# Index scores as three fp32r products instead of one fp32 product, in a hybrid encoder layer on one Trainium2 core

## The chip, the cores and the metric

The kernel runs on one core of one Trainium2 chip. The metric is the device time of one execution in microseconds (us). TensorE is the matrix engine, VectorE, ScalarE and GpSimd compute element by element, and SyncE (SP) issues most of the DMA transfers. "PEld" in the profile is TensorE's weight load, which can overlap its matmuls.

## What is computed

One inference step of one layer on 1,024 prompt tokens and 128 sample tokens (8 sequences of 16). The reference, cut to what matters:

```python
h = RMSNorm_pre(x) * (1 + scale) + shift
z = h @ W_in                      # (1152, 2048) @ (2048, 5712)
q, k, v, iq, ik, iw, za, u, zs = split(z)
# indexer, block of 128 queries; 16 heads of 64; limit is block-causal by 64 tokens
s = einsum('bqhd,bsd->bqhs', iq, ik) * 64 ** -0.5
score = einsum('bqhs,bqh->bqs', relu(s), iw)
score = where(visible, score, -inf)
_, idx = top_k(score, 256)
# grouped-query attention over the chosen keys
attn = softmax(q @ gather(k, idx)) @ gather(v, idx)
# S5: 64 groups, 64 complex states each, scan over positions, y = Re(C h) + D u
y_ssm = gelu(s5(u)); y_ssm = y_ssm * sigmoid(y_ssm @ w_glu + b_glu)
out = concat(attn * silu(za), y_ssm * silu(zs)) @ W_out
y = x + gate * RMSNorm_post(out)
```

Queries among the first 256 tokens see at most 256 keys and need no choice, so index scores are computed for the query tiles 2 to 7 (tiles of 128 tokens), each against the keys up to its own end.

## The kernel before, in words

The program has two parts, `project_in` (about the first two thirds of the time) and `mix_tokens`. Only `project_in` is changed.

**The projection.** W_in is cut into 45 blocks of up to 128 output columns. Tokens go in two passes: the first has 768 tokens (two slices of 384), the second 384 tokens (one slice). The weights of a block come in two halves of 8 contraction blocks. So the work is a list of 180 half-blocks, called halves here: numbers 0 to 89 are the first pass, and NA = 90 to NA+89 the second. Every product of the projection is split: three fp32r matmuls, high by high, low by high and high by low (lines 1598 to 1600), 48 in a half of the first pass and 24 in one of the second. ScalarE copies a weight half to fp32r (`high`, line 983), VectorE subtracts that copy from the weights (`low`, line 1259); GpSimd does the subtraction in part of the second pass (line 817, `POOL_LOW`). In the first pass the split of half n+1 stands at the head of half n's work on ScalarE and VectorE, in the second the split of half n+2.

**What runs beside it.** Each engine goes through the same loop over halves and does extra work at fixed numbers. TensorE inserts work behind given products (`beside`, "spots"). The order is written by hand, as constants:

- `TILE_AT[t] = (first half, how many)` places index tile t. In its first halves TensorE does the score products, a pair of heads at a spot: 5 spots a half in the first pass (behind products 1, 4, 7, 10, 13) and 3 in the second (1, 4, 7). A pair is two heads on the upper and the lower 64 rows of the array (`score_pair`, line 1672), each in its own PSUM bank `ps_s`. ScalarE takes the relu (`relu`, line 1012) into one of two places of `rel`, VectorE multiplies by the head's weight and adds it to `score` (`add_scores`, lines 1420 and 1423). The remaining halves of the tile are for the search: 32 rounds of MAX8 and MATCH_REPLACE8 on VectorE (`choose`, lines 1435 and 1437) share them evenly (`rounds_in`), and a mask is kept at the end (line 1442).
- A score matmul waits until the unit two before it has had its relu. A relu waits until the unit two before it has been added.
- Eight batches of the scan run in the second pass, from half NA+7 on, one in 6 halves (`scan_at`). Batch b has its inputs multiplied in its halves 0 and 1 (line 1696), VectorE turns and scans them (lines 1221 to 1252), and its outputs are multiplied in halves 6 and 7 (lines 1715 and 1720). Tables `toep` and `q_mat` for the outputs are in two buffers and are loaded by `load_outputs` at offset 7 of the batch; inputs, with `p_in` and `rot`, by `load_inputs` at offset 5.
- SP issues the loads of the weights. Its iteration n starts once the half whose buffer it takes is done: 4 halves behind n in the first pass, 8 in the second. All other DMAs stand between them, in the same queue.
- The keys and values needed by the next part are loaded by `load_results` after half NA+71's weights and turned by TensorE in halves NA+70, NA+72 and so on (`turn_rows`).

The fp32 score matmul shows in the trace as two matmul records with two weight loads.

## Time and profile before

| | |
|---|---|
| median of 3 runs | 2257.27 us (2253.56 to 2257.91) |
| the profiled execution's own time | 2255.91 us |
| span of the profiled execution | 2254.0 us |
| TensorE busy | 2150.6 us, 95% |
| VectorE busy | 1268.4 us, 56% |
| ScalarE busy | 737.4 us, 33% |
| GpSimd busy | 449.0 us, 20% |
| first pass, halves 2 to 89 | about 120 to 977 us of the span |
| second pass, halves NA to NA+89 | 977 to 1486 us |
| score matmuls | 352 records, between 411 and 1380 us |

Times in the rows are microseconds from the span's start unless marked ns. A timeline row gives the start, the duration, engine, line, operation and tiles; "x4" at its end merges four instructions, and brackets hold the idle time before it and what ended it. Matmuls are pipelined, so a record's duration is longer than its distance from the next. Granted clock is that of TensorE, as a share of full speed.

### The profile page before, as it was taken

To read this page: it belongs to the slowest core of one execution; us is meant where nothing else is said; L and a number is where in the kernel's file an instruction comes from. 1 tells how busy PE (TensorE), PEld (TensorE's weight loads), DVE (VectorE), ACT (ScalarE), POOL (GpSimd) and SP (SyncE) were. 2 spreads that over 40 slices of the span, in tenths; PEclk is the share of its full clock that TensorE was granted. 3 is DMA by queue.
4 is the path that set the end of the run, shared out by engine and by line. 5 is a ranking of instruction groups with operands and counts; after the bars stand their busy time and mean duration, and the time that the engine had idled before them with its cause. 6 is when DMAs were issued, how large, how long until landed. Compare 5 with 4: busy or idle time off the path is not lost. (4 is left out here: it accounts for less than half of the span.)

```text
span 2254.0 us, 33185 instructions
## 1 busy us (share of the span) xinstructions
PE 2150.6 (95%) x13028; PEld 1869.8 (83%) x13028; DVE 1268.4 (56%) x2292; ACT 737.4 (33%) x1324; POOL 449.0 (20%) x654
## 2 busy tenths in 40 slices
PE   5899999999999998999999999989999989999898
PEld 3489999888898898999976977979777777887786
DVE  4228433577778693335547988955567553223353
ACT  5221222222322323332223234553355542222241
POOL 0001332792000000203333445620000000000100
PEclk9999999999999999999999999999999999999999
DMA  9954556344454335377764645544411222224653
GB/s 368 379 116 108 151 156 172 99 117 117 128 129 114 98 112 174 87 183 211 222 216 127 179 117 174 164 136 134 109 50 48 87 72 87 77 80 151 232 182 117
DMA packets 432381, 325.80 MB, mean 145 GB/s; under 512 B 122937, under 2 KB 377441, under 8 KB 430681
## 3 DMA queue, kind: packets, MB, share of 16 engines
q1 hardware_dynamic: 427618, 303.75, 46.4%
q0 software_dynamic: 4176, 16.78, 2.1%
q10 hardware_dynamic: 432, 3.15, 0.4%
q8 instruction: 104, 1.70, 0.3%
q14 instruction: 51, 0.42, 0.1%
HBM read 264.52 MB, written 63.28 MB: 145 GB/s over the span
## 5 line engine op out<-in xcount | busy, mean ns | idle before, releaser
L1598 PE MATMUL ps_z<-h_hi_a,w_hi 128*128 128x384 f32 (+1 forms) x1408 | 484.5, 344 | 1.4 <-DVE w_lo L1259 1.4
L1600 PE MATMUL ps_z<-h_hi_a,w_lo 128*128 128x384 f32 (+1 forms) x1408 | 472.5, 336 | 0.0
L1599 PE MATMUL ps_z<-h_lo_a,w_hi 128*128 128x384 f32 (+1 forms) x1408 | 471.5, 335 | 0.0
L1259 DVE TENSOR_TENSOR w_lo<-w_raw,w_hi 128x1024 fp32r<-128x1024 f32 (+1 forms) x135 | 185.0, 1374 | 362.1 <-ACT w_hi L983 361.6
L1598 PEld LDWEIGHTS ps_z<-h_hi_a,w_hi 128*128 128x128 f32 (+1 forms) x1408 | 263.2, 187 | 32.3 <-issue 27.1
L1599 PEld LDWEIGHTS ps_z<-h_lo_a,w_hi 128*128 128x128 f32 (+1 forms) x1408 | 263.5, 187 | 0.8
L1600 PEld LDWEIGHTS ps_z<-h_hi_a,w_lo 128*128 128x128 f32 (+1 forms) x1408 | 263.2, 187 | 0.9
L983 ACT ACTIVATE w_hi<-w_raw 128x1024 fp32r<-128x1024 f32 (+1 forms) x180 | 186.2, 1052 | 228.6 <-PE ps_z L1600 223.0
L1598 PE MATMUL ps_z<-h_hi_b,w_hi 128*128 128x384 f32 (+1 forms) x720 | 251.1, 349 | 0.6 <-DVE w_lo L1259 0.4
L1600 PE MATMUL ps_z<-h_hi_b,w_lo 128*128 128x384 f32 (+1 forms) x720 | 242.9, 337 | 0.0
L1599 PE MATMUL ps_z<-h_lo_b,w_hi 128*128 128x384 f32 (+1 forms) x720 | 242.6, 337 | 0.0
L2789 DVE TENSOR_TENSOR o_lo<-o_raw,o_hi 128x512 fp32r<-128x512 f32 x114 | 78.6, 691 | 220.3 <-ACT o_hi L2733 220.2
L1003 ACT ACTIVATE z_sb<-ps_z 128x384 f32<-128x384 f32 (+1 forms) x85 | 50.9, 600 | 343.1 <-PE ps_z L1600 343.1
L1598 PEld LDWEIGHTS ps_z<-h_hi_b,w_hi 128*128 128x128 f32 (+1 forms) x720 | 135.7, 188 | 32.4 <-issue 28.1
L2733 ACT ACTIVATE o_hi<-o_raw 128x512 fp32r<-128x512 f32 x114 | 71.7, 631 | 247.2 <-PE ps_l L2937 96.9
L817 POOL TENSOR_TENSOR w_lo<-w_raw,w_hi 128x1024 fp32r<-128x1024 f32 x45 | 110.8, 2465 | 175.4 <-ACT w_hi L983 175.4
L1599 PEld LDWEIGHTS ps_z<-h_lo_b,w_hi 128*128 128x128 f32 (+1 forms) x720 | 135.9, 189 | 0.4
L1600 PEld LDWEIGHTS ps_z<-h_hi_b,w_lo 128*128 128x128 f32 (+1 forms) x720 | 135.8, 189 | 0.4
L1435 DVE MAX8 top<-score_a 128x8 f32<-128x384 f32 (+3 forms) x128 | 97.2, 759 | 3.4
L1423 DVE SCALAR_TENSOR_TENSOR score_a<-rel_a,iw,score_a 128x384 f32<-128x384 f32 (+2 forms) x105 | 67.0, 639 | 50.0 <-ACT rel_a L1012 43.8
L1437 DVE MATCH_REPLACE8 score_a<-top,score_a 128x384 f32<-128x384 f32 (+3 forms) x128 | 95.0, 742 | 0.0
L826 POOL TENSOR_TENSOR z_sb<-z_sb,sig_a 128x768 f32<-128x768 f32 x16 | 29.5, 1842 | 315.8 <-ACT sig_a L1001 315.8
(508 smaller groups left out, 3848.2 us busy)
## 6 DMA issues: line engine op xcount, KB each, us to landing
w_raw<-in_w_in SPq DMA_DIRECT2D x176, 512.0 KB, 4.1
wada<-in_w_ada SPq DMA_DIRECT2D x32, 1024.0 KB, 14.2
o_raw<-in_w_out SPq DMA_DIRECT2D x114, 256.0 KB, 3.0
wg<-in_w_ada SPq DMA_DIRECT2D x32, 512.0 KB, 6.3
zt<-z_sb SPq DMA_DIRECT2D x36, 384.0 KB, 4.7
slabs<-in_x_prompt POOLq DMA_DIRECT2D x8, 1024.0 KB, 7.8
zt<-z_sb SPq DMA_DIRECT2D x36, 192.0 KB, 4.0
out_y_prompt<-out_rows POOLq DMA_DIRECT2D x10, 512.0 KB, 4.8
```

The source lines that it names most:

```text
L817: G.tensor_tensor(w_lo[r][:, :, 0:m], w_raw[r][:, :, 0:m], w_hi[s][:, :, 0:m].bitcast(F32), ALU.subtract).then_inc(w_lo_pool, 1)
L983: A(w_hi[s][:, :, 0:m], w_raw[r][:, :, 0:m], ACT.Copy).then_inc(w_hi_ok, 1)
L1003: A(dst, src, ACT.Copy).then_inc(z_read, 1)
L1259: V.tensor_tensor(w_lo[r][:, :, 0:m], w_raw[r][:, :, 0:m], w_hi[s][:, :, 0:m].bitcast(F32), ALU.subtract).then_inc(w_lo_ok, 1)
L1423: V.scalar_tensor_tensor(out, rel(t)[:, u % 2, 0:w], wgt, out, ALU.mult, ALU.add).then_inc(s_acc, 1)
L1435: V.max(top8[:], score(t)[:, 0:keys]).then_inc(top, 1)
L1437: V.match_replace(score(t)[:, 0:keys], top8[:], score(t)[:, 0:keys], CHOSEN).then_inc(top, 1)
L1598: M(out, hi, H_HI[p][:, kk, cols], start=kk == 0, stop=False)
L1599: M(out, hi, H_LO[p][:, kk, cols], start=False, stop=False)
L1600: return M(out, lo, H_HI[p][:, kk, cols], start=False, stop=kk == KB - 1)
L2733: A(hi, raw, ACT.Copy).then_inc(w_hi_ok, 1)
L2789: V.tensor_tensor(lo, raw, hi.bitcast(F32), ALU.subtract).then_inc(w_lo_ok, 1)
```

## The change

Three things are changed together.

1. The index scores of the prompt are computed as the projection's products are: queries and keys are each split into an fp32r copy and a rest, and each pair of heads gets six fp32r matmuls instead of two fp32 ones. ScalarE makes the copies (`queries_high`) and VectorE the rests (`queries_low`), in the half before the tile starts, the keys once for the first pass and once for the second. The rests overwrite the fp32 queries and keys. A pair now waits once, until both units of the pair before have had their relu.
2. The tables `toep` and `q_mat` are held once instead of twice, which makes room for the copies of the second pass. Their load waits for the outputs of the batch before and stands at offset 10 instead of 7.
3. The pieces of keys per tile are listed by hand: those of the fourth tile are 384 and 256 wide instead of 320 twice. Tile 2 goes from halves 32 to 39 to halves 34 to 40, tile 3 from 40 to 49 to 41 to 49, tile 6 from NA+36 to NA+59 to NA+38 to NA+59. Tiles 4, 5 and 7 stay. The loads of queries, and that of the results, move by some iterations.

```diff
-TILE_AT = {2: (32, 8), 3: (40, 10), 4: (50, 12), 5: (62, 14), 6: (NA + 36, 24), 7: (NA + 60, 30)}
-PIECES_OF = {2: 1, 3: 2, 4: 2, 5: 2, 6: 2, 7: 2}
+TILE_AT = {2: (34, 7), 3: (41, 9), 4: (50, 12), 5: (62, 14), 6: (NA + 38, 22), 7: (NA + 60, 30)}
+SCORE_PIECES = {2: [(0, 384)], 3: [(0, 256), (256, 256)], 4: [(0, 384), (384, 256)], 5: [(0, 384), (384, 384)],
+                6: [(0, 448), (448, 448)], 7: [(0, 512), (512, 512)]}
...
-        q_mat = then("q_mat", [P, 2, PAIR_BATCH, 2, P])
-        toep = then("toep", [P, 2, U_BATCH, P])
+        q_mat = then("q_mat", [P, PAIR_BATCH, 2, P])
+        toep = then("toep", [P, U_BATCH, P])
+        iq_hi_b, ik_hi_b = then("iq_hi_b", [P, IDX_HEADS // 2, P], F32R), then("ik_hi_b", [P, SEQ], F32R)
...
-                after(sp, y_mm, 2 * (b - 1))
-                sp.dma_start(toep[:, b % 2], scr["toep"][:, b * U_BATCH:b * U_BATCH + U_BATCH]).then_inc(t_land, 16)
-                sp.dma_start(q_mat[:, b % 2], scr["s5_out"][:, js]).then_inc(q_land, 16)
+                after(sp, y_mm, 2 * b)
+                sp.dma_start(toep[:], scr["toep"][:, b * U_BATCH:b * U_BATCH + U_BATCH]).then_inc(t_land, 16)
+                sp.dma_start(q_mat[:], scr["s5_out"][:, js]).then_inc(q_land, 16)
...
+                sp.wait_ge(s_mm, UNIT0[7] + IDX_HEADS * PIECES_OF[7])
...
-                    if n == TILE_AT[t][0] + 2:
+                    if n == TILE_AT[t][0]:
                         load_queries(t)
...
-                for b in scans(n, 7):
+                for b in scans(n, 10):
                     load_outputs(b)
...
-                if n == ROWS_AT + 1:
+                if n == ROWS_AT + 3:
                     load_results()
...
-                if n == TILE_AT[6][0] + 6:
+                if n == NA + 42:
                     load_queries(6)
-                if n == TILE_AT[7][0] + 4:
+                if n == NA + 52:
                     load_queries(7)
...
+            def queries_high(t):
+                if t == 2:
+                    act.wait_ge(ik_in, 32)
+                    act.wait_ge(taps_out, 16 * BATCHES)
+                    A(ik_hi_a[0][:], ikT_a[:, 0:KEYS_HIGH], ACT.Copy).then_inc(idx_hi, 1)
+                    A(ik_hi_a[1][:], ikT_a[:, KEYS_HIGH_FROM:A_TOK], ACT.Copy).then_inc(idx_hi, 1)
+                if t == 6:
+                    act.wait_ge(ik_in, 64)
+                    A(ik_hi_b[:], ikT_b[:], ACT.Copy).then_inc(idx_hi, 1)
+                act.wait_ge(iq_in, 16 * (IDX_TILES.index(t) + 1))
+                A(iq_hi(t)[:], iqT(t)[:], ACT.Copy).then_inc(idx_hi, 1)
...
+                for i in IDX_TILES:
+                    if n == TILE_AT[i][0] - 1:
+                        queries_high(i)
...
+            def queries_low(t):
+                if t == 2:
...
+                if t == 6:
+                    dve.wait_ge(idx_hi, queries_split(6) - 1)
+                    V.tensor_tensor(ik_lo_b[:], ikT_b[:], ik_hi_b[:].bitcast(F32), ALU.subtract).then_inc(idx_lo, 1)
+                dve.wait_ge(idx_hi, queries_split(t))
+                V.tensor_tensor(iq_lo(t)[:], iqT(t)[:], iq_hi(t)[:].bitcast(F32), ALU.subtract).then_inc(idx_lo, 1)
...
+                if n in (TILE_AT[2][0], TILE_AT[6][0]):
+                    weights_ready(p)
...
+                for i in IDX_TILES:
+                    if n == TILE_AT[i][0] - 1:
+                        queries_low(i)
...
-                if n in (TILE_AT[2][0], TILE_AT[6][0]):
-                    weights_ready(p)
...
                 if r == 0:
-                    pe.wait_ge(iq_in, 16 * (IDX_TILES.index(t) + 1))
-                    pe.wait_ge(ik_in, 32 if t < 6 else 64)
+                    pe.wait_ge(idx_lo, queries_split(t))
...
-                for h2 in range(2):
-                    u = UNIT0[t] + 2 * r + h2
-                    after(pe, s_relu, u - 1)
-                    half = slice(64 * h2, 64 * h2 + 64)
-                    M(ps_s[u % 2][:, 0:w], iqT(t)[half, hp, :], ikT(t)[half, c:c + w], start=True, stop=True).then_inc(s_mm, 1)
+                u = UNIT0[t] + 2 * r
+                after(pe, s_relu, u)
+                halves = (slice(0, 64), slice(64, 128))
+                for h2, half in enumerate(halves):
+                    M(ps_s[h2][:, 0:w], iq_hi(t)[half, hp, :], ik_hi(t, c, w)[half], start=True, stop=False)
+                for h2, half in enumerate(halves):
+                    M(ps_s[h2][:, 0:w], iq_lo(t)[half, hp, :], ik_hi(t, c, w)[half], start=False, stop=False)
+                for h2, half in enumerate(halves):
+                    M(ps_s[h2][:, 0:w], iq_hi(t)[half, hp, :], ik_lo(t)[half, c:c + w], start=False, stop=True).then_inc(s_mm, 1)
```

## Rows read from the trace of the kernel before

**Rows 1.** The page, busy tenths of VectorE in 40 slices of the span.
```profile
DVE  4228433577778693335547988955567553223353
```

**Rows 2.** Timeline of TensorE, a pair 256 wide in half 41.
```profile
501.32 0.34 PE L1600 MATMUL ps_z<-h_hi_a,w_lo 128*128 128x384 f32 x1
501.59 0.70 PE L1672 MATMUL ps_s<-ikT_a,iqT_a 64*128 64x256 f32 x4
...
502.50 0.34 PE L1599 MATMUL ps_z<-h_lo_a,w_hi 128*128 128x384 f32 x1
```

**Rows 3.** Timeline of TensorE, a pair 512 wide in half NA+61.
```profile
1347.56 0.34 PE L1600 MATMUL ps_z<-h_hi_b,w_lo 128*128 128x384 f32 x1
1347.83 1.13 PE L1672 MATMUL ps_s<-ikT_b,iqT_b 64*128 64x512 f32 x4
...
1349.17 0.34 PE L1599 MATMUL ps_z<-h_lo_b,w_hi 128*128 128x384 f32 x1
```

**Rows 4.** Timeline of TensorE, two fp32r products on 64 rows.
```profile
1877.04 0.39 PE L2937 MATMUL ps_t<-o_hi,attn_lo 128*128 128x512 f32 x1
1877.36 0.49 PE L2925 MATMUL ps_t<-gpost,sel 64*128 64x512 f32 x1
...
1878.36 0.40 PE L2936 MATMUL ps_l<-o_lo,attn_hi 128*128 128x512 f32 x1
```

**Rows 5.** Scan outputs on line 1720; durations in ns, min/median/max, first and last start.
```profile
L1720 PEld LDWEIGHTS ps_k<-hist,q_mat x256: 182/187/187, 1044.0 to 1313.8; 64*128 64x128 f32 x128
...
L1720 PE MATMUL ps_k<-hist,q_mat x16: 282/283/387, 1108.8 to 1109.7; 64*128 64x144 f32 x16
```

**Rows 6.** Timeline of TensorE, the first products of halves 45 and 50.
```profile
544.79 0.33 PE L1598 MATMUL ps_z<-h_hi_a,w_hi 128*128 128x384 f32 x1
...
588.68 0.44 PE L1598 MATMUL ps_z<-h_hi_a,w_hi 128*128 128x384 f32 x1
```

**Rows 7.** Timeline, VectorE's search of tile 3 and the start of tile 4.
```profile
565.18 1.22 DVE L1259 TENSOR_TENSOR w_lo<-w_raw,w_hi 128x1024 fp32r<-128x1024 f32 x1
...
567.83 0.69 DVE L1435 MAX8 top<-score_a 128x8 f32<-128x512 f32 x1
...
569.34 0.69 DVE L1435 MAX8 top<-score_a 128x8 f32<-128x512 f32 x1
...
573.78 1.22 DVE L1259 TENSOR_TENSOR w_lo<-w_raw,w_hi 128x1024 fp32r<-128x1024 f32 x1
...
593.06 1.23 DVE L1259 TENSOR_TENSOR w_lo<-w_raw,w_hi 128x1024 fp32r<-128x1024 f32 x1
...
595.17 1.46 PE L1672 MATMUL ps_s<-ikT_a,iqT_a 64*128 64x320 f32 x4
595.33 0.44 ACT L1012 ACTIVATE rel_a<-ps_s 128x320 f32<-128x320 f32 x1 [0.22 <-DVE score_a L1423]
```

**Rows 8.** Busy time: stretch, length, PE, PEld, DVE, ACT, POOL; clock, DMA, GB/s.
```profile
1339.00:1345.00 6.00, 5.74 (x12) 3.28 (x14) 3.02 (x5) 2.95 (x5) 1.15 (x1) 0.50 0.30 86
```

**Rows 9.** Scan inputs of the third batch: issue, landing, first use.
```profile
1065.37 0.43 SPq L598 DMA_DIRECT2D p_in<-s_in  x1
...
DMA to landing us min/median/max: 5.7/5.7/5.7
...
1072.48 0.47 PE L1696 MATMUL ps_p<-uy,p_in 128*64 128x144 f32 x4
```

**Rows 10.** Tile 6's start and search and tile 7's start; first row as rows 8.
```profile
1250.00:1328.00 78.00, 75.18 (x491) 72.04 (x490) 76.39 (x114) 20.18 (x31) 40.55 (x43) 1.00 0.65 183
...
1170.08 1.87 PE L1672 MATMUL ps_s<-ikT_b,iqT_b 64*128 64x448 f32 x4 [4.60 <-DMA iqT_b<-zt]
...
1232.54 1.09 DVE L1435 MAX8 top<-score_b 128x8 f32<-128x896 f32 x1
...
1338.03 0.48 DVE L1420 TENSOR_SCALAR score_b<-rel_b,iw 128x512 f32<-128x512 f32 x1
...
1339.26 2.93 PE L1672 MATMUL ps_s<-ikT_b,iqT_b 64*128 64x512 f32 x4 [3.42 <-ACT rel_b L1012]
```

More of the change, by code:

```diff
@@ L161 @@
     UNIT0[_t] = sum(IDX_HEADS * PIECES_OF[_s] for _s in IDX_TILES if _s < _t)
-def score_width(tile):
-    return (tile + 1) * P // PIECES_OF[tile]
 def score_pairs(tile):
-    w = score_width(tile)
-    return [(hp, c * w) for hp in range(IDX_HEADS // 2) for c in range(PIECES_OF[tile])]
+    return [(hp, c, w) for hp in range(IDX_HEADS // 2) for c, w in SCORE_PIECES[tile]]
 def pair_spots(n):
@@ L1714, in scan_outputs @@
                         group = 2 * (2 * half + j) + g
-                        M(bank(j, g), toep[:, b % 2, group, :], uy[:, b % 3, group, :], start=j == 0, stop=False)
+                        M(bank(j, g), toep[:, group, :], uy[:, b % 3, group, :], start=j == 0, stop=False)
                 for j in range(2):
@@ L1719, in scan_outputs @@
                             rows = slice(64 * g, 64 * g + 64)
-                            ins = M(bank(j, g), q_mat[rows, b % 2, 2 * half + j, ri, :], hist[rows, b % 2, ri, 2 * half + j, :],
+                            ins = M(bank(j, g), q_mat[rows, 2 * half + j, ri, :], hist[rows, b % 2, ri, 2 * half + j, :],
                                     start=False, stop=ri == 1 and j == 1)
```

33 lines of the change are left out of this document (27 added, 6 removed).

## The prediction

> **What bounds the kernel now.** I read the page first. TensorE is busy nearly throughout, so a microsecond is won or lost where TensorE's own stream changes or where it stops. VectorE is busy 70 to 90% in the stretches in which index tiles are scored and searched [rows 1]; that is the second thing to watch. In the timeline of TensorE a pair of score products (two heads, one per row half) sits among the projection products. Without it those start 0.1775 us apart; around a pair 256 wide the distance from the product before to the second product after is 1.18 us, so the pair costs 1.18 - 2 x 0.1775 = 0.82 us [rows 2]. At 512 wide it is 1.61 - 0.36 = 1.25 us [rows 3]. The slope, 0.43 us over 256 columns, is 4 array cycles per column at 2.4 GHz: the two heads already run beside each other, and 0.40 us is fixed. Then the timeline of VectorE in the search of tile 3: what counts there is how far it lies behind TensorE at the start of each half.
>
> **The products, per part.** Each pair becomes three rounds (high by high, low by high, high by low), each of one column per cycle. Is an fp32r product on 64 rows as dear in fixed cost? The gate unit of the last stage does two, one behind the other: 1.32 us from the product before to the second after, less 2 x 0.226 of ordinary distance (213 ns of columns and 13) and 2 x 0.213 of columns leaves 0.44 us [rows 4]. So I keep 0.40 us. A round costs w/2.4 ns plus some 13 ns (fp32r products of 384 columns start 173 ns apart where undisturbed, 160 by columns). New pair: 256 wide 0.76, 384 wide 0.91, 448 wide 1.00, 512 wide 1.08 us, against 0.82, 1.04, 1.15, 1.25, and 0.93 for the 320 that tile 4 has now. Tiles 2 to 5: 8 x 0.12 + 16 x 0.07 + (14.9 - 8 x 0.91 - 8 x 0.76) + 16 x 0.12 = 5.5 us less. Tiles 6 and 7 give 16 x 0.15 and 16 x 0.17 less, used below.
> Rounds 256 wide last 107 ns and need two weight loads. Matmuls 144 wide on alternate row halves start 0.12 us apart, a load of 128 columns each [rows 5]: 16 in 0.9 us, so two loads fit into 0.12 us. I take that row. One load by itself lasts 0.187 us [rows 5]; if a round had to wait for a whole one, the gain of tiles 2 to 5 would be gone (+0.6 instead of -5.5).
> The Trainium skill (TensorE: Matmul & The Clock Gate, LDWEIGHTS) puts a load at columns divided by 1.2, 107 ns here. Two in sequence would make every round at least 0.21 us, and tiles 2 to 5 would cost about 5 us more than now. The rows at 0.12 us for two loads speak against it; no fp32r pair on both halves is in this trace.
>
> **VectorE in the first pass.** Tiles 2 and 3 now have 5 halves for their 32 search rounds instead of 6, since each starts later and the next one is not moved as far. Tile 3: a round takes 1.52 us, a weight split adds 1.0 (8.60 us from one split to the next with 5 rounds) [rows 7]. A half lasts 8.45 or 9.0 us; five take 43.89 us from half 45 to half 50 [rows 6]. Before: 5 or 6 rounds a half, 8.6 to 10.1 us. VectorE's split started 4.38 us after half 50 began (593.06 - 588.68), and TensorE's third score pair had to wait 0.8 us for the relus that the adds had delayed (last relu 595.33 + 0.44) [rows 6, 7]. Two units of relu output exist, so two pairs pass and the third stops until two adds are done, 2.7 us after that split starts.
> After: rounds 6, 6, 7, 6, 7. With lag 1.3 us at half 45, each half adds its work less its length: 1.3 + 10.1 - 9.0 = 2.5; + 10.1 - 8.45 = 4.1; + 11.6 - 9.0 = 6.8; + 10.1 - 8.45 = 8.5. In half 49 the split for half 50 ends at 8.5 + 1.2, 0.8 us after half 50 should begin: TensorE waits. Then come the split of the queries (1.0), seven rounds and the mask: lag 11.8 us. Third pair released at 11.8 + 2.7 = 14.5, reached at 5.8: 8.7 us. Together 9.5, less the 0.8 of now: **+8.7** (bounds +5 and +10). The same recursion with the old counts gives 4.3 us of lag at half 50, measured 4.38.
> Tile 2 (1.25 us a round, low work slowed while GpSimd computes the rotations): lag 6.4 us at half 41 against 2.7 now, third pair late by **+2.8** (0 to +4). Tile 4 keeps its halves but has the query split of tile 5 in its last one: **+0.8**. ScalarE's copies (1.05 us per tile, 2.1 for keys) stand behind the weight copy of their half with over 3 us in hand: nothing.
> A TensorE stop is followed by half clock: after the stop that ends at 1339.26 the granted clock of 1339 to 1345 is 0.50 [rows 8, 10]. The stop before half 50's third pair is longer than that one, the clock should fall to 1.2 GHz for 3.4 us of work or so: **+1.7** (0 to +3).
>
> **The scan tables held once.** Their loads go out three iterations later on SP's queue, so they wait for nothing new, and are on chip several us before use. But they now stand one iteration ahead of the next batch's inputs: 1 MB in the same queue. Inputs of the third batch: issued at 1065.37, landed 5.7 us later at 1071.1, TensorE uses them at 1072.48 [rows 9]. Weight block, u and inputs are 1.6 MB in some 6.8 us from the first issue, 340 GB/s once under way, so 1 MB more directly ahead is 3 us. The slack of the second to fifth batch is 2.4, 1.4, 1.7 and 3.0 us; with the y stores and u stores between, the delay is 3, 3, 2 and 1 us: stops of 0.8, 1.7, 0.3 and 0, **+2.8** (0 to +7). Later batches lie where TensorE waits for VectorE anyway.
>
> **Second pass.** Now tile 6 stops at its first pair for its queries (4.6 us) [rows 10], and again at halves NA+39 and NA+40 behind the scan's work on VectorE. Starting at NA+38 instead of NA+36 the queries, even with 3 us of extra queue and 2.3 us of splits, come in time: half NA+44 begins 8.9 us earlier: the stop with the half clock behind it is 6.8 us, cheaper pairs give 2.4, a wait for two relus where it was one takes 0.3. But VectorE has no idle time from 1250 to 1328 (76.4 of 78 us) [rows 10], and it bounds this stretch: its first round started at 1232.54 and the first add of tile 7 at 1338.03 [rows 10]. Rounds of NA+42 and NA+43 that used to fill idle time move behind NA+44. From NA+44 on: 2.9 us until its scan inputs are read, 32 rounds x 2.32 = 74.2, mask 0.7, 1.0 for the queries of tile 7, and other work 25.7: of the 105.5 us between those two rows rounds and mask are 74.9, idle time 2.4, the inputs read in NA+43 and one split 2.5. So the first add comes 104.5 us after NA+44 begins, 96.4 now. So of 8.9 us only 0.8 are left there. Tile 7: its third pair starts now at 1339.26 and takes 2.93 us in two pieces [rows 10]; with both relus awaited at once it ends 1 us earlier; its other 13 pairs give 2.2 us. **-4.0** (-11 if VectorE were not the bound, +1). Behind it the k/v loads are issued two iterations later and land some 1.7 us before their use: nothing.
>
> **Sum**: -5.5 + 8.7 + 2.8 + 0.8 + 1.7 + 2.8 - 4.0 = +7.3 us. On the profiled execution's own 2255.91 us (span 2254.0 and 1.9 around it) that is 2263.2. The median of the three runs, 2257.27, lies 1.36 above this execution, so I state 2264.5. 0.2% is 4.5 us, about what a measurement of this kernel tells from no change.
>
> **Rivals.**
> Forecast, 0.62: as worked out, 2260 to 2270.
> Faster, 0.12: VectorE's backlog never reaches TensorE's third pair in halves 41 and 50, so that the +14 us of stops and clock don't arise: -5.5 + 2.8 - 4.0 = -6.7, 2250.6. It decides at lag 3 us at the start of half 50; for it speaks only that waits of this kind are small now (0.8 us), against it that the lag is 4.38 us with a sixth half.
> Cancelled, 0.14: the same mechanism but with half the stops (clock not lost, the inputs of the scan in time): -5.5 + 8 - 4.0 + 0 to 4, 2256 to 2260.
> Loads bound the rounds, 0.06: one 0.187 us load per round, 6.1 us more than the forecast: 2271. By the skill's 107 ns per load, two in sequence, it would be about 2276.
> Row halves don't run beside each other in fp32r, 0.06: 6 cycles per column instead of 3, or 2 more than now. 33,792 pair columns x 2 / 2.4 = +28 us instead of a gain of 10: 2303. Against it: in fp32 they do, at 4 cycles per column for two heads [rows 2, 3].
> That the change does less than it says (products still in two slower passes) would show as four records per pair; projection products on the same type show one record each [rows 2].
>
> **Chances.** Of the forecast 0.05 falls within 0.2%, 0.57 beyond; of "cancelled" 0.13 within. Slower 0.57 + 0.06 + 0.06 + 0.01 = 0.70, same 0.18, faster 0.12. The range leaves out the faster rival and the row halves: 2252 to 2276. The forecast's own range is 2260 to 2270.
>
> **What would show it.** Right: six records per pair in 0.76 to 1.1 us; a stop of 8 to 9 us at the third pair of half 50 with half clock behind it; 2 to 4 us at half 41; no wait for the queries of tile 6, but a wait at tile 7's third pair as long as before; waits of 1 to 2 us for the scan inputs. Wrong: no stop at half 50, or pairs above 1.3 us.

## The result, and the profile after

| | before | after |
|---|---|---|
| median of the runs compared | 2257.59 us (2253.56 to 2259.03, 6 runs) | 2275.74 us (2272.49 to 2281.93, 6 runs) |
| profiled execution, its own time | 2255.91 us | 2272.49 us |
| span | 2254.0 us | 2270.7 us |

The ratio is 1.0085 [1.0069, 1.0102]: slower, as forecast and inside the range, but by 18 us where I had worked out 7. The page of after, busy tenths of VectorE in 40 slices of the span; where [rows 1] has 7777 (slices 9 to 12, 454 to 681 us) stands 8686. VectorE, searching tiles 3 and 4 there, is fuller in some slices and emptier in others:

```profile
DVE  4227442486868694235457998965567553223343
```

**Where the time went.** I added up the distances between the first projection products of the halves (TensorE's timeline, in us):

| halves | before | after | difference |
|---|---|---|---|
| 31 to 39, tile 2 | 88.04 | 86.87 | -1.2 |
| 40 to 44, tile 3's pairs | 57.08 | 62.23 | +5.2 |
| 45 to 54, tile 3's search and tile 4's pairs | 103.50 | 114.19 | +10.7 |
| 55 to 79 | 238.11 | 235.79 | -2.3 |
| 80 | 13.83 | 16.67 | +2.8 |
| NA+7 to NA+26, first scan batches | 111.91 | 114.73 | +2.8 |
| NA+35 to NA+59, tile 6 | 168.77 | 167.98 | -0.8 |
| NA+60 to NA+69, tile 7's pairs | 71.73 | 72.27 | +0.5 |

Halves 0 and 1 together take 0.7 us less and the first starts 1.0 earlier; the other halves agree within 0.1 us. What lies behind the halves takes 768.3 us against 767.6; its code is the same in all kernels here, and over their traces it varies from 765.9 to 775.2. Together this makes the 16.7 us between the spans. In half 80 TensorE waits 3.5 us for VectorE in both kernels, and behind this wait the granted clock was 1.00 before and 0.50 (904 to 909 us) after. Whether that is the change's doing stays open: run e13 below, whose code is the same up to there, has 13.85 us, but of the 13 traces with fp32r pairs ten have 15.1 us or more, and the four with fp32 pairs (before, e2, e3, e11) all have 13.8.

**The pair is as cheap as forecast.** The timeline of TensorE after, a pair 256 wide in tile 3 (counterpart of [rows 2]). Two heads stand in each record ("x2"):

```profile
513.42 0.34 PE L1647 MATMUL ps_z<-h_hi_a,w_lo 128*128 128x384 f32 x1
513.69 0.39 PE L1717 MATMUL ps_s<-ik_hi_a,iq_hi_a 64*128 64x256 f32 x2
513.91 0.28 PE L1719 MATMUL ps_s<-ik_hi_a,iq_lo_a 64*128 64x256 f32 x2
514.03 0.28 PE L1721 MATMUL ps_s<-ik_lo_a,iq_hi_a 64*128 64x256 f32 x2
...
514.53 0.34 PE L1646 MATMUL ps_z<-h_lo_a,w_hi 128*128 128x384 f32 x1
```

By the same working as before: 1.11 - 0.355 = 0.76 us (forecast 0.76), and a pair 512 wide, around which the same distance is 1.46 us (1388.79 to 1390.25), takes 1.11 us (forecast 1.08; the median of the 16 such pairs is 1.09). The last two rounds of 256 columns start 0.12 us apart with two weight loads each, so neither rival about the loads or the row halves came true. The Trainium skill (TensorE: Matmul & The Clock Gate, LDWEIGHTS) puts a load of 128 columns at 107 ns, columns divided by 1.2. That two loads follow one another, which makes 0.21 us, was my reading of it and not the page's word; the 0.12 us decide against this reading for two loads on different row halves. My sentence on [rows 5] has a slip: 16 matmuls in 0.9 us start 0.06 us apart, and it is two of them that fit into 0.12 us, as the sum then uses it.

**The stops.** The timeline of after around the third pairs of tile 3 (half 41) and tile 4 (half 50). In brackets stands the idle time before the instruction and who ended it:

```profile
488.71 2.26 POOL L820 TENSOR_TENSOR turns<-turns,turn_work 128x504 f32<-128x504 f32 x1
...
489.76 2.30 DVE L1453 TENSOR_TENSOR iq_lo_a<-iqT_a,iq_hi_a 128x1024 fp32r<-128x1024 f32 x1
...
493.20 0.33 PE L1645 MATMUL ps_z<-h_hi_a,w_hi 128*128 128x384 f32 x1
...
501.14 1.22 DVE L1292 TENSOR_TENSOR w_lo<-w_raw,w_hi 128x1024 fp32r<-128x1024 f32 x1
502.29 0.49 DVE L1464 TENSOR_SCALAR score_a<-rel_a,iw 128x256 f32<-128x256 f32 x1
...
503.89 0.51 PE L1717 MATMUL ps_s<-ik_hi_a,iq_hi_a 64*128 64x256 f32 x2 [4.83 <-ACT rel_a L1042]
...
591.42 1.89 POOL L844 TENSOR_TENSOR z_sb<-z_sb,sig_a 128x768 f32<-128x768 f32 x1 [15.60 <-ACT sig_a L1019]
591.53 2.86 DVE L1453 TENSOR_TENSOR iq_lo_a<-iqT_a,iq_hi_a 128x1024 fp32r<-128x1024 f32 x1
...
591.67 0.44 PE L1645 MATMUL ps_z<-h_hi_a,w_hi 128*128 128x384 f32 x1 [0.72 <-DVE w_lo L1292]
...
594.44 0.44 PE L1717 MATMUL ps_s<-ik_hi_a,iq_hi_a 64*128 64x384 f32 x2 [1.45 <-DVE iq_lo_a L1453]
...
605.38 1.23 DVE L1292 TENSOR_TENSOR w_lo<-w_raw,w_hi 128x1024 fp32r<-128x1024 f32 x1
606.52 0.41 DVE L1464 TENSOR_SCALAR score_a<-rel_a,iw 128x384 f32<-128x384 f32 x1
...
608.19 0.69 PE L1717 MATMUL ps_s<-ik_hi_a,iq_hi_a 64*128 64x384 f32 x2 [8.85 <-ACT rel_a L1042]
```

Both stops name ScalarE's relu, but ScalarE had waited for a place in `rel_a`, and VectorE frees one only when it adds. It adds at 502.29 and 606.52, once the search, the mask and a weight split are behind it. The chain is the forecast one. Its lengths aren't: 4.83 us, and 8.85 with another 1.45 at the first pair and 0.72 at the start of half 50. The rows at 493.20 and 591.67 are the first products of halves 41 and 50; the weight split at the head of VectorE's work for the same halves starts at 501.14 and 605.38, so VectorE lies 7.9 and 13.7 us behind. Note the query split: 2.30 and 2.86 us, where the same instruction takes 1.2 undisturbed and I had put in 1.0.

The windows of after, columns as in [rows 8] (the granted clock is the number ahead of the last two). The clock was at 0.50 behind the stop at half 41. In half 50 TensorE did nothing from 600 to 606 us, and the clock was at 0.50 from 603 to 613:

```profile
504.00:507.00 3.00, 3.00 (x13) 2.78 (x14) 1.34 (x3) 1.04 (x3) 2.69 (x9) 0.50 0.00 0
...
600.00:603.00 3.00, 0.00 (x0) 0.00 (x0) 2.86 (x7) 0.00 (x0) 0.00 (x0) 1.00 0.00 0
603.00:606.00 3.00, 0.00 (x0) 0.00 (x0) 2.86 (x6) 0.00 (x0) 0.00 (x0) 0.50 0.00 0
606.00:610.00 4.00, 1.81 (x8) 1.38 (x9) 2.30 (x5) 1.22 (x4) 0.00 (x0) 0.50 0.01 4
610.00:613.00 3.00, 3.00 (x11) 2.56 (x11) 1.24 (x2) 0.42 (x2) 0.00 (x0) 0.50 0.00 0
613.00:616.00 3.00, 3.00 (x22) 2.37 (x20) 0.97 (x2) 0.66 (x2) 0.00 (x0) 0.96 0.00 0
```

At 0.50 TensorE gets through 11 products in 3 us, at 0.96 through 22. Of the low stretch of 10 us, the first 5 (until 608.19) fall on the stop itself and cost nothing.

The second pass, TensorE's waits from 1165 to 1375 us (engine, tile and line; who ended it; us in total, times, longest):

```profile
PE ps_s L1717 <- DVE iq_lo_b L1453: 6.8, 1, 6.8
PE ps_s L1717 <- ACT rel_b L1042: 6.7, 2, 3.8
PE ps_p L1745 <- DVE part L1261: 4.2, 1, 4.2
PE ps_z L1645 <- DVE w_lo L1292: 2.8, 2, 2.7
```

The queries of tile 6 are no longer waited for (4.60 us in [rows 10]). In return tile 7, whose third pair had waited 3.42 us [rows 10], now waits at its **first** pair for 6.80 us, since its query split stands on VectorE among the last rounds of tile 6's search. VectorE's chain is also longer than I had worked out. Half NA+44 begins at 1249.67, the first round of the search starts at 1254.14, and the first add of tile 7 comes at 1357.03, 107.4 us after NA+44 begins (104.5 forecast):

```profile
1249.67 0.33 PE L1645 MATMUL ps_z<-h_hi_b,w_hi 128*128 128x384 f32 x1
...
1254.14 1.09 DVE L1479 MAX8 top<-score_b 128x8 f32<-128x896 f32 x1
...
1357.03 0.48 DVE L1464 TENSOR_SCALAR score_b<-rel_b,iw 128x512 f32<-128x512 f32 x1
```

The windows show VectorE full and the clock down:

```profile
1347.00:1357.00 10.00, 5.12 (x17) 3.94 (x19) 9.75 (x14) 1.44 (x3) 3.31 (x2) 0.50 0.17 52
```

And at the scan's third batch TensorE waits for its inputs, which [rows 9] had had 1.4 us in hand (a row of the timeline, then the window behind it, columns as in [rows 8]):

```profile
1087.15 0.47 PE L1745 MATMUL ps_p<-uy,p_in 128*64 128x144 f32 x4 [2.02 <-issue]
...
1087.00:1091.00 4.00, 3.85 (x23) 3.49 (x24) 1.61 (x6) 0.00 (x0) 0.00 (x0) 0.58 0.75 214
```

"issue" means that the profile shows nothing that the wait was for; that it was the inputs is shown by e2 and e5.

### The profile page after: what moved, and what is told of

The parts are those of the page before. It is cut to its first block and busy times, and to the rows that moved or that the text cites. A ratio compares the mean times of both kernels' runs of the same rounds, so it can differ in the third digit from the quotient of the medians.

```text
span 2270.7 us, 33554 instructions
## 1 busy us (share of the span) xinstructions
PE 2139.8 (94%) x13204; PEld 1889.6 (83%) x13204; DVE 1286.9 (57%) x2301; ACT 744.7 (33%) x1333; POOL 448.6 (20%) x654
## 5 line engine op out<-in xcount | busy, mean ns | idle before, releaser
L1292 DVE TENSOR_TENSOR w_lo<-w_raw,w_hi 128x1024 fp32r<-128x1024 f32 (+1 forms) x135 | 189.6, 1409 | 374.3 <-ACT w_hi L1001 373.8
L1467 DVE SCALAR_TENSOR_TENSOR score_a<-rel_a,iw,score_a 128x384 f32<-128x384 f32 (+1 forms) x105 | 64.1, 612 | 47.3 <-ACT rel_a L1042 41.3
```

The lines of the kernel that those rows point to most:

```text
L1292: V.tensor_tensor(w_lo[r][:, :, 0:m], w_raw[r][:, :, 0:m], w_hi[s][:, :, 0:m].bitcast(F32), ALU.subtract).then_inc(w_lo_ok, 1)
```

## The experiments

Fifteen kernels. Ratios are to the kernel before, run on the same chip, with 95% intervals; the changed kernel itself stands at 1.0085. 0.1% is 2.26 us. Where I give microseconds of a difference between two ratios, that is what they are.

### Which part of the change costs, first pass

**e1**, the changed kernel with the halves of before for tiles 2 and 3.

```diff
-TILE_AT = {2: (34, 7), 3: (41, 9), 4: (50, 12), ...
+TILE_AT = {2: (32, 8), 3: (40, 10), 4: (50, 12), ...
```

> The changed kernel with the searches of tiles 2 and 3 put back to where the kernel before has them (tile 2 from half 32 over 8 halves, tile 3 from half 40 over 10); the three split products, the pieces and all else stay. Theory (the third pair of a tile stops TensorE while VectorE still ends the search of the tile before, and a stretch at the lower granted clock follows): the stops of 4.83 us at half 41 and 8.85 us at half 50 go, together with the 3.4 and 10.2 us at a granted clock of 0.50 behind them, so about 14 us less than the changed kernel (11 to 18): 2261 us, ratio to the kernel before 1.0016. Rival 1 (the split work on VectorE and ScalarE, or the products' form, costs the time, wherever the tiles lie): within 3 us of the changed kernel, 2273 to 2278 us. Rival 2 (the stop moves on to the pair behind): half of it, about 2268 us.

Measured: 2266.26 us, ratio 1.0049 [1.0037, 1.0061], 8 us less than the changed kernel. The theory holds in direction; on its size the medians and the trace differ. In the trace halves 40 to 54 together take 14.3 us less than in the changed kernel, as expected, but the part behind the halves takes 775.2 us instead of 768.3 with the same code. The intervals of the two ratios leave room from 2 to 15 us, so the medians don't decide the size. One stop stays even with the long searches, at the third pair of tile 3, which the kernel before hasn't.

```profile
488.13 1.95 DVE L1292 TENSOR_TENSOR w_lo<-w_raw,w_hi 128x1024 fp32r<-128x1024 f32 x1
490.00 1.36 DVE L1464 TENSOR_SCALAR score_a<-rel_a,iw 128x256 f32<-128x256 f32 x1
491.47 1.28 DVE L1467 SCALAR_TENSOR_TENSOR score_a<-rel_a,iw,score_a 128x256 f32<-128x256 f32 x1
...
493.28 0.53 PE L1717 MATMUL ps_s<-ik_hi_a,iq_hi_a 64*128 64x256 f32 x2 [2.05 <-ACT rel_a L1042]
...
489.07 2.14 POOL L819 TENSOR_TENSOR turns<-turns,turn_work 128x504 f32<-128x504 f32 x1
491.17 1.30 POOL L820 TENSOR_TENSOR turns<-turns,turn_work 128x504 f32<-128x504 f32 x1
```

The weight split lasts 1.95 us, and the two adds 1.36 and 1.28, which take 0.35 and 0.48 elsewhere. The first add ends when GpSimd's operation of 489.07 is over (491.21) and 0.15 more have passed, the second 0.28 us after the operation of 491.17 has ended (492.47). So where GpSimd happens to be decides about 2.5 us of VectorE's time at a place where TensorE has none in hand.

**e3**, the kernel before with only the shortened searches (the fp32 products stay).

```diff
-TILE_AT = {2: (32, 8), 3: (40, 10), 4: (50, 12), ...
+TILE_AT = {2: (34, 7), 3: (41, 9), 4: (50, 12), ...
```

> The kernel before with one thing of the change: tile 2 from half 34 over 7 halves and tile 3 from half 41 over 9; the products stay single fp32 ones. Theory (the shortened searches leave VectorE behind at the third pair of the next tile): a stop at half 41 and one at half 50, each with a stretch at the lower clock behind it; since the fp32 pairs arrive about 0.2 us later each, the stops are 1 us or so smaller than in the changed kernel: +10 us over the kernel before (7 to 15), about 2267 us, ratio 1.0044. Rival (the stops belong to the three products or to the split work): +2 us at most.

Measured: 2266.52 us, ratio 1.0053 [1.0037, 1.0068], +12 us. The shorter searches alone cost nearly two thirds of the whole (in the traces 10.3 us over halves 40 to 54, of 15.8). But the two stops aren't alike:

```profile
500.80 1.29 PE L1672 MATMUL ps_s<-ikT_a,iqT_a 64*128 64x256 f32 x4 [0.27 <-ACT rel_a L1012]
...
601.79 2.09 PE L1672 MATMUL ps_s<-ikT_a,iqT_a 64*128 64x320 f32 x4 [6.67 <-ACT rel_a L1012]
```

At tile 4, 6.67 us against the changed kernel's 8.85 and 1.45; at tile 3, 0.27 against 4.83. So the stop at half 41 needs the split work or the sooner products as well. By the rows: VectorE's first add came at 499.78 here and at 502.29 there (2.5 us, a query split of 2.30 in between); the pair was due at 500.53 and at 499.06 (1.5 us); and there it waits for both banks (0.6 us by the rows; e12 below doesn't bear this term out). Together 4.6. Most of the 1.5 us is that half 41 itself begins 1.3 us earlier (493.20 against 494.48).

**e14** tests that: no low parts at all, so its scores are those of the high parts alone.

```diff
-                for i in IDX_TILES:
-                    if n == TILE_AT[i][0] - 1:
-                        queries_low(i)
...
-                    M(ps_s[h2][:, 0:w], iq_lo(t)[half, hp, :], ik_hi(t, c, w)[half], start=False, stop=False)
...
-                    M(ps_s[h2][:, 0:w], iq_hi(t)[half, hp, :], ik_lo(t)[half, c:c + w], start=False, stop=True).then_inc(s_mm, 1)
```

> The changed kernel without the low parts: VectorE's splits of the queries and keys and the second and third product of each pair are left out (the scores are then those of the high parts alone), ScalarE's high parts stay. It takes apart the 4.83 us at the third pair of tile 3 (0.27 us in run e3, which has the same halves and single products). By the rows, 2.5 us of it are VectorE's subtraction of the queries (2.30 us) in front of the search's last rounds, 1.5 us that the third pair is due sooner, 0.6 us that it waits for both banks. Theory: here the third pair is due another 0.5 us sooner and VectorE ends 2.3 us sooner, so the wait at half 41 is about 3 us, and the one at half 50 7.5 to 8.5 us; the pairs cost 0.5 us instead of 0.75 to 1.09. Rival (the split's subtraction has room, and the wait is the products' alone): 5 us or more at half 41.

Measured: 2241.03 us, ratio 0.9941 [0.9926, 0.9956]. Timeline:

```profile
497.80 0.38 PE L1714 MATMUL ps_s<-ik_hi_a,iq_hi_a 64*128 64x256 f32 x2 [1.07 <-ACT rel_a L1042]
595.17 0.69 PE L1714 MATMUL ps_s<-ik_hi_a,iq_hi_a 64*128 64x384 f32 x2 [8.19 <-ACT rel_a L1042]
```

1.07 us at half 41 where I expected 3, and 8.19 at half 50, as expected. The rival (5 us or more) falls. Without the low parts most of the stop at half 41 goes, more than my sum has it: the first add came at 496.34, 5.95 us sooner than in the changed kernel, and the pair was due at 496.73, 2.33 sooner; 3.6 us of the 4.83 are so gone, 2.30 of them the query split. Of the rest, 0.4 us is a weight split that took 1.62 us and takes 1.22 here, and VectorE already lies 1.5 us less behind when half 40 begins. What that comes from isn't traced.

**e12**, the changed kernel with the first product of a pair waiting for its own bank only.

```diff
-                after(pe, s_relu, u)
                 halves = (slice(0, 64), slice(64, 128))
                 for h2, half in enumerate(halves):
+                    after(pe, s_relu, u + h2 - 1)
```

> The changed kernel with one edit: the first product of a pair waits only for its own bank (the relu before last) as in the kernel before, the second for the other; the changed kernel waits for both before the first. Theory (the backlog, not the form of the wait, sets the stops): the last product of the pair ends when it did, under 1 us less in all, ratio to the kernel before 1.008. Rival (waiting for both banks at once is what makes the third pair late, 4.83 us at half 41 where the single products have next to none): 3 us or more faster.

Measured: 2270.19 us, ratio 1.0067 [1.005, 1.0085]. The interval touches that of the changed kernel. In the traces halves 41 and 50 take 19.62 and 25.63 us here, 19.23 and 25.41 in the changed kernel: the form of the wait isn't what makes the stops, and the rival (3 us or more) has nothing in these halves. Whether something is gained elsewhere stays open: the ratios differ by 0.18%, 4 us, and their intervals overlap.

**e8**, the changed kernel with tile 3's search one half longer.

```diff
-TILE_AT = {2: (34, 7), 3: (41, 9), 4: (50, 12), 5: (62, 14), ...
+TILE_AT = {2: (34, 7), 3: (41, 10), 4: (51, 12), 5: (63, 14), ...
```

> The changed kernel with tile 4 from half 51 and tile 5 from half 63 (12 and 14 halves as before), so that tile 3's search has one half more; tile 2 and all else stay. Theory (the 8.85 us stop at the third pair of tile 4 and the 10.2 us at a granted clock of 0.50 behind it are VectorE's backlog from tile 3's search): half 50 loses the stop, about 12 us less than the changed kernel (9 to 14), ratio to the kernel before 1.003; the stop at half 41 stays at 4 to 5 us. Rival (not the search but the split or ScalarE hold the pair): the stop moves to half 51 with the same length.

Measured: 2265.00 us, ratio 1.0035 [1.0023, 1.0047], 11 us less than the changed kernel. In its trace halves 45 to 54 take 103.5 us, as before the change, instead of 114.2. One half of 9 us given to VectorE takes away the 8.85 us stop, the split's 1.45 us and the time at the lower clock; a wait of 2.75 us stays at tile 4's third pair. It is the clearest run for the forecast's main term. The stop at half 41 stays, 4.7 us.

### The tables and the scan

**e2**, the kernel before with the tables' loads at their new place (two buffers kept), and **e5**, the changed kernel with them behind the next inputs.

```diff
-                after(sp, y_mm, 2 * (b - 1))
+                after(sp, y_mm, 2 * b)
...
-                for b in scans(n, 7):
+                for b in scans(n, 10):
```

> The kernel before with one thing of the change: the loads of the scan's output tables are issued three halves later and wait for the last products of the batch before; both buffers and all else stay. Theory (the later tables' loads stand ahead of the next batch's input loads in SyncE's queue and make TensorE wait for the inputs of batches 1 to 3): +3 to +5 us over the kernel before, in the halves NA+13, NA+19 and NA+25, about 2261 to 2262 us, ratio 1.0018. Rival (the stops seen at the scan of the changed kernel come from something else, such as the split of tile 6): ratio 1.0000 within 0.0005.

```diff
-                for b in scans(n, 10):
+                for b in scans(n, 11):
                     load_outputs(b)
```

> The changed kernel with the loads of the output tables issued one half later, so that they stand behind the next batch's input loads in SyncE's queue. Theory (inputs held up by the tables ahead of them): TensorE's waits for the scan's inputs at halves NA+13 and NA+19 go, about 4.5 us less than the changed kernel (2 to 6), 2271 us, ratio to the kernel before 1.006. Rival (not the queue): no difference; and if the tables themselves now come too late for the outputs, a new wait at the output products makes it slower than the changed kernel.

Measured: e2 2259.11 us, ratio 1.0021 [1.001, 1.0032], +4.7 us; e5 2270.33 us, ratio 1.0070 [1.0058, 1.0083], 3.4 us less than the changed kernel. In the trace of e2 halves NA+13 and NA+19 are 0.6 and 1.8 us longer, and TensorE waits 6.3 us for tile 6's queries instead of 4.60 [rows 10]; in that of e5 NA+13 and NA+19 are back at before's 7.87 us. The waits follow the order of the queue; a load one place further back costs nothing, as the tables have time.

### The second pass

**e4**, the changed kernel with tile 6 at its old halves.

```diff
-... 6: (NA + 38, 22), 7: (NA + 60, 30)}
+... 6: (NA + 36, 24), 7: (NA + 60, 30)}
```

> The changed kernel with tile 6 from half NA+36 over 24 halves, as before the change. Theory (the second pass of tile 6 is bound by VectorE, so where its pairs start matters little): a wait for the queries of 4 to 9 us comes back at NA+36, and the waits at NA+41 to NA+53 shrink by as much, for VectorE starts its adds some 4 us sooner: within 3 us of the changed kernel. Rival (the later start was the gain): 6 us or more slower than the changed kernel. Rival 2 (the later start is what costs): 4 us or more faster.

Measured: 2278.70 us, ratio 1.0095 [1.0081, 1.0108], 2 us more than the changed kernel. TensorE waits 9.2 us for the queries' low part at NA+36; the halves NA+35 to NA+39 are 18 us longer than in the changed kernel, and NA+41 to NA+60 give 13.6 of it back. By the medians that is the theory's case, that VectorE decides and not the start. But the medians differ by 2 us and the profiled executions by 7, so how much the later start is worth isn't settled between the theory and the rival.

**e7**, the changed kernel with tile 7's queries split three halves earlier (the same edit on ScalarE and on VectorE).

```diff
-                    if n == TILE_AT[i][0] - 1:
+                    if n == TILE_AT[i][0] - (4 if i == 7 else 1):
```

> The changed kernel with one edit: the split of tile 7's queries (ScalarE's and VectorE's part) three halves earlier in both programs. In the changed trace TensorE waits 6.80 us at NA+60 for that split, which stands behind the search of tile 6 on VectorE. Theory 1 (VectorE is the bound there, the split only the place where the wait shows): the first pair comes 6.8 us sooner, but a wait of 3 to 6 us for the rel buffers stands at the third pair instead; 0 to 4 us less than the changed kernel, with the low-clock stretch behind it shorter. Theory 2 (the split's place is the cost): 7 us or more less, no wait left at NA+60 and NA+61.

Measured: 2274.08 us, ratio 1.0080 [1.0068, 1.0092]. TensorE's waits from 860 to 1400 us:

```profile
PE ps_s L1717 <- ACT rel_b L1042: 17.4, 7, 7.5
```

The wait for the split is gone from the list, and a wait of 7.5 us for the relus has taken its place. Theory 1: the split's place shows the wait, VectorE's load makes it.

**e13**, the changed kernel with tile 7 two halves later and tile 6's search two halves longer.

```diff
-... 6: (NA + 38, 22), 7: (NA + 60, 30)}
+... 6: (NA + 38, 24), 7: (NA + 62, 28)}
```

> The changed kernel with tile 6 over 24 halves from NA+38 and tile 7 from NA+62 over 28: the search of tile 6 has two halves more, and tile 7 starts two halves later; nothing else moves. Theory (TensorE reaches tile 7's first pair before VectorE has ended the search of tile 6, and two halves of 4.2 us each in between cover it): the 6.80 us at NA+60 and most of the low-clock stretch of 10.2 us behind it go, 8 us less than the changed kernel (5 to 11), ratio to the kernel before 1.005. Rival (the search of tile 7, two halves shorter, stops TensorE later, or the halves' own low parts wait for VectorE, as at NA+53): under 3 us less.

Measured: 2268.14 us, ratio 1.0059 [1.0043, 1.0076], 6 us less than the changed kernel (5 to 11 expected). Tile 7's wait has gone from 6.80 to 4.4 us, that at NA+53, where a projection product waits for its own low part behind the search, from 2.7 to 4.2, and that at NA+50 from 4.2 to 1.0. Of 13.7 us of waits 4.1 are gone.

### Towards a better kernel

**e6** has at once: tile 2 over 9 halves, tile 3 from 41 over 10, tile 4 from 51, tile 5 from 63, the tables as in e5, tile 7's split as in e7.

```diff
+TILE_AT = {2: (32, 9), 3: (41, 10), 4: (51, 12), 5: (63, 14), 6: (NA + 38, 22), 7: (NA + 60, 30)}
```

> The changed kernel with everything that the theory blames put right at once: tile 2 from half 32 over 9 halves, tile 3 from half 41 over 10, tile 4 from half 51, tile 5 from half 63 (each search one half longer or as long as before), the output tables' loads behind the next inputs' loads, and tile 7's queries split three halves earlier. Theory: against the changed kernel the stop at half 41 and that at half 50 go with the low-clock stretches behind them (18 us in the changed trace, of which the same stops of the kernel before were about 1), the scan's 4.5 us go, and about 3 of the 6.80 us at NA+60: in all 20 to 25 us less than the changed kernel, 2251 to 2256 us, ratio to the kernel before 0.9985 (0.996 to 1.001). Rival (the split work itself costs VectorE about 1.2 to 2.7 us a tile, and the stops only move on to the next tile): 2262 us or more, no better than the run with the halves of before and the tables' order mended.

Measured: 2257.11 us, ratio 1.0006 [0.9993, 1.0018]: 18 us less than the changed kernel, and just as fast as before, at the bad end of the ratios that I expected. Halves 40 to 44 take 55.77 us (before: 57.08), so here the cheaper products arrive. A stop of 2.8 us stays at half 51, and the second pass is as in the changed kernel.

**e9** adds GpSimd's work to it, **e11** the same to the kernel before.

```diff
-POOL_LOW = [n >= NA + 56 or (n >= NA + 34 and n % 2 == 1) for n in range(NHALF)]
+POOL_LOW = [n >= NA + 44 or (n >= NA + 34 and n % 2 == 1) for n in range(NHALF)]
```

> The kernel of run e6 (shifted halves, tables behind the inputs, tile 7's split earlier) with one edit: the low parts of the weights are made by GpSimd in every half from NA+44 on, instead of every second one up to NA+56. VectorE loses six subtractions of 1.8 us in the stretch where it is busy 77.1 of 80 us. Theory (VectorE's load is what stops TensorE between NA+44 and NA+61): of the waits left there (4.2 us at NA+50, 2.7 at NA+53, about 7.5 at NA+60 and NA+61) about 9 us go, with part of the lower clock: 8 us less than run e6 (5 to 12), ratio to the kernel before 0.997. Rival (GpSimd, or its port shared with VectorE, gives it back: GpSimd's subtraction takes 2.5 us and stands in front of its scan steps): within 2 us of run e6.

> The same edit on the kernel before: low parts of the weights on GpSimd in every half from NA+44 on. Theory (VectorE was the bound there already before the change, so the products' gain could not arrive): the waits of 2.2 us at NA+50 and 3.4 us at NA+61 shrink, 4 us less than before (1 to 7), ratio 0.998. If run e9 gains more than this one does, the change's gain of the second pass is set free by it. Rival: no difference in either.

Measured: e9 2256.29 us, ratio 1.0003 [0.999, 1.0015], no gain over e6; e11 2249.73 us, ratio 0.9971 [0.9961, 0.9982], 6.5 us less than before. The rival holds for e9. The groups of VectorE's instructions from the start of half NA+44 to the mask of tile 6, first in e6 (1229.2 to 1335.7 us), then in e9 (1234.8 to 1341 us):

```profile
L1479 DVE MAX8 top<-score_b 128x8 f32<-128x896 f32 x32 | 34.9, 1091 | 0.8
...
L1292 DVE TENSOR_TENSOR w_lo<-w_raw,w_hi 128x1024 fp32r<-128x1024 f32 x5 | 10.0, 2000 | 3.6 <-ACT w_hi L1001 3.6
L1280 DVE TENSOR_TENSOR part<-rot,wide 128x512 f32<-128x512 f32 x4 | 6.9, 1768 | 0.0
L1273 DVE TENSOR_TENSOR_SCAN wide<-s_tabs,wide 128x128 f32<-128x128 f32 x16 | 5.3, 402 | 0.1
...
L1453 DVE TENSOR_TENSOR iq_lo_b<-iqT_b,iq_hi_b 128x1024 fp32r<-128x1024 f32 x1 | 1.2, 1215 | 0.0
```

```profile
L1479 DVE MAX8 top<-score_b 128x8 f32<-128x896 f32 x32 | 34.9, 1091 | 0.8
...
L1280 DVE TENSOR_TENSOR part<-rot,wide 128x512 f32<-128x512 f32 x4 | 7.8, 1996 | 0.0
L1273 DVE TENSOR_TENSOR_SCAN wide<-s_tabs,wide 128x128 f32<-128x128 f32 x16 | 7.5, 537 | 0.1
L1453 DVE TENSOR_TENSOR iq_lo_b<-iqT_b,iq_hi_b 128x1024 fp32r<-128x1024 f32 x1 | 3.2, 3212 | 0.0
L1284 DVE TENSOR_TENSOR last<-part 128x4 f32<-128x4 f32 x2 | 3.2, 1590 | 0.2
...
L1254 DVE COPY dec_b<-ps_p 128x32 f32<-128x32 f32 x3 | 0.6, 185 | 4.8 <-PE ps_w L1745 4.8
```

VectorE has 10.0 us of subtractions less, and the other instructions on two tiles take 0.9, 2.2, 2.0 and (L1284, 0.3 us in e6) 2.9 us more: 8.0 us given back beside GpSimd's longer work. Another 1.2 us goes into idle time: before its first round VectorE now waits 4.8 us for TensorE's scan inputs, where in e6 it waited 3.6 for ScalarE's copy. The search's own instructions keep their time to the nanosecond. So the mask comes 106.2 us after half NA+44 begins instead of 106.5, and TensorE, which got there sooner, waits 10.2 us at tile 7's third pair instead of 7.5. In e11 the scan operations pay 2.2 us too, but there is no query split in their way, and more of the relief stays.

**e10** is e9 with longer searches, and **e15** is e10 with the low parts shared as in the changed kernel.

```diff
+TILE_AT = {2: (32, 9), 3: (41, 11), 4: (52, 12), 5: (64, 14), 6: (NA + 38, 24), 7: (NA + 62, 28)}
...
+                    if n == TILE_AT[i][0] - (6 if i == 7 else 1):
```

> The kernel of run e9 with each search that is still late given more halves: tile 3 from half 41 over 11, tile 4 from half 52, tile 5 from half 64, tile 6 from half NA+38 over 24, tile 7 from NA+62 over 28, its queries split six halves ahead. Theory: the 2.8 us stop at half 51 goes, and what run e9 leaves at NA+60; 3 to 6 us less than run e9, about 2243 to 2247 us, ratio to the kernel before 0.995. Rival (the search of tile 7, now over 22 halves, holds up what follows it): no gain, or a new wait behind NA+70.

> The kernel of run e10 with the weights' low parts shared between VectorE and GpSimd as in the changed kernel. It tells which of the two edits brought run e10 its 12 us below the kernel before. Theory (the halves given to the searches did; GpSimd's share alone changed nothing in run e9): within 4 us of run e10, ratio 0.996. Rival (both are needed, because VectorE is busy 78 of 80 us there): 8 us or more above run e10, ratio 0.998 or more.

Measured: e10 2243.28 us, ratio 0.9945 [0.9931, 0.996]; e15 2244.08 us, ratio 0.9950 [0.9937, 0.9963]. Both beat both kernels, by 12 us the one before and by 32 us the changed one, and they don't differ: the halves given to the searches did it, not GpSimd (against e6, e15 changes only these halves and splits tile 7's queries two halves further ahead). How much of the 12 us the cheaper products bring isn't shown, as no run gives the same longer searches to the kernel before. In e10 TensorE waits once between 410 and 780 us, for 0.4 us.

## Where the prediction was right, and where it was wrong

The direction and the mechanism were right: VectorE's backlog stops TensorE at the third pair of a tile. The size was wrong: 7.3 us stood for 16.6 in the profiled executions and 18 between the medians. The terms that failed are VectorE's lag at half 41 (6.4 us, measured 7.9), the split of the queries (1.0, measured up to 2.86), the time to tile 7's first add (104.5, measured 107.4), and the lower clock, which was charged behind the stop of half 50 alone and also followed those of 4.83 and 2.0 us.

**Right: the products.** 0.76 and 1.11 us against the forecast 0.76 and 1.08; halves 31 to 39 gave 1.2 us (1.0 forecast). In e6 and e10 halves 40 to 44, too, are 1.3 us shorter than before.

**Right in kind and close in size: tile 3 to 4.** Forecast +8.7 for the stops and +1.7 for the clock, less 1.5 for the pairs: 8.9. Measured 10.7 in halves 45 to 54, and e8 takes all of it away with one half. The stops are 0.72, 1.45 and 8.85 us, 11.0 together, where 9.5 had been worked out. The step that was short is "the split of the queries (1.0)": it took 2.86 us, because GpSimd's operation had started 0.11 us earlier, and VectorE's lag became 13.7 us instead of 11.8. The 3.4 us of work at the lower clock come from no row; measured are 4.8 (608.19 to 613), which at half speed cost 2.4 us.

**Wrong size: tile 2 to 3.** Forecast +2.8, less 1.1 for the pairs; measured +5.2, that is 6.3 against 2.8 for the stop and its clock. Two steps failed. The first is "lag 6.4 us at half 41": it was 7.9 (493.20 to 501.14). The pair was reached 5.9 us after the half began and released 10.7 after it, as the recipe of the prediction has it for this lag, and that is the 4.83 us. (For its own 6.4 us the recipe gives 3.3, not 2.8.) The prediction has "low work slowed while GpSimd computes the rotations", but puts the new subtraction at 1.0 us; here it took 2.30. In e3, where there is no such subtraction, the lag is 4.2 us and the wait 0.27; in e14, without the low parts, 3.8 and 1.07. The second is the clock: the prediction charges it behind the stop of half 50 alone, and here, at 0.50 from 504 to 507 us, it is the other 1.5 us.

**Right in sum by luck: the scan.** Forecast +2.8 in the halves of batches 1 to 3, measured +2.8 over NA+7 to NA+26; but NA+13 and NA+19 alone are 4.5 us longer, and 1.7 less in NA+7, which also varies between runs of the same code (7.5 us here, 9.1 in e13), hides it. The waits themselves are as forecast, 0.8 and 2.0 us (0.8 and 1.7); not charged was the clock behind the second. The mechanism is shown from both sides, by e2 (+4.7 us, of which 2.3 at tile 6's queries in NA+36) and e5 (-3.4 us).

**Right: tile 6 bound by VectorE.** "So of 8.9 us only 0.8 are left there": NA+35 to NA+59 gave 0.8.

**Wrong: tile 7.** Forecast -3.2 (third pair 1 us earlier, cheaper pairs 2.2), measured +0.5. The step that failed is "So the first add comes 104.5 us after NA+44 begins": it came after 107.4, 2.9 us later. Of these, 1.6 are that the search starts 4.5 us into NA+44 and not 2.9, VectorE having stood idle for 3.6 us until ScalarE's copy of a weight half; the rest lies in operations with two inputs, such as the four of line 1280, which took 6.9 us where their counterparts took 3.7 before. I had also let the third pair be held as before and forgot that the split of tile 7's queries is awaited by its **first** pair. TensorE stood 6.80 us in one piece instead of 3.42. But e7 shows that moving the split alone is of no use, the wait is then 7.5 us at the third pair: it is VectorE's lateness that counts. e13 shows that two halves more are worth 6 us.

**Open:** 2.8 us in half 80 of the profiled execution, for which the prediction has no term. With it, and the smaller terms above, the profiled 16.6 us stand against the forecast 7.3: 3.5 for half 41, 1.8 for half 50, 3.7 for tile 7, 2.8 for half 80, less 2.5 in the rest (the stop of +0.8 that I expected between tiles 4 and 5 isn't there, and the start is earlier).

The two rivals with less stopping fell with the stops of 8.85 and 4.83 us. That the range held was luck: its upper end, 2276, was there for weight loads in sequence, which did not come true, and the median is 0.3 us below it.

## What to carry to other kernels

When a schedule is tight between an engine that searches and an engine that multiplies, a cheaper product isn't worth anything by itself: it brings TensorE sooner to the same wait. Give the slower chain more room first (here one or two halves per tile, with the tables' loads and tile 7's split moved as well, turned +0.85% into -0.5%), and then count the saving. A forecast of a stop should carry the stretch at the lower clock behind it: here some 1.5 us for stops of 2.0 and 4.83 us. When new work goes to an engine's queue, ask who is first to wait for it, not only how long it takes, and price it beside what its neighbour does at that moment.

## What the runs showed of the hardware

- **VectorE and GpSimd hold each other up, a whole instruction at a time.** The query split is one instruction of 128x1024. It took 1.22 us in e1 and 2.30 and 2.86 in the changed kernel. Both times an operation of GpSimd had started before it, and the split ended 1.1 us after that operation did: at 594.39, with GpSimd's operation running from 591.42 to 593.31, and at 492.06, with GpSimd's from 488.71 to 490.97. It had waited for nearly all of it. MAX8 and MATCH_REPLACE8 never show this, in e9 as little as in e6. The Trainium skill (SBUF — State Buffer, SBUF: two separate sides) says that the port pair shared by the two is an exclusive lock, held for the whole instruction, against VectorE operations with two SBUF inputs or in a two-port mode. The trace agrees. e9 shows what this costs over a stage: of 10.0 us taken off VectorE 8.0 came back.
- **The last two of the three rounds of two fp32r products on both row halves start 0.12 us apart at 256 columns**, with two weight loads in each. The fixed cost of a pair, about 0.4 us, is the same as for one fp32 product, whether it is split in three or not.
- **The clock at a stop.** The granted clock was 0.50 from 603 to 613 us, with the 8.85 us stop ending at 608.19, and from 1339 to 1345 behind the 3.42 us stop of [rows 10]. Not every stop has it: the 3.5 us wait in half 80 of the kernel before ends in a stretch (894 to 904 us) at 1.00, and so "a TensorE stop is followed by half clock" is too general. What matters is how much of the stretch falls on work: behind the 8.85 us stop TensorE did 11 products in 3 us instead of 22.
